# Outputs and forget gathers moved into attention's middle, the prefix scan cut into pieces, and the first RWKV loads issued during the last attention pair

## Chip, core and metric

The kernel runs on one core of one Trainium2 chip. The metric is the device time of one execution in microseconds (us); the time of a version is the median of its runs. Engines are named as in the profile: PE (matmul), PEld (its weight loads), DVE, ACT, POOL, SP (whose queue here only issues DMAs), and the core's 16 DMA engines.

## The reference

One step of a hybrid decoder layer with four mixers side by side. The prompt has 2048 tokens, the decode batch 8 sequences of 4 tokens with 8192 cached tokens each. What the change touches, cut to it:

```python
z = rmsnorm(x) @ w_in                       # 1024 -> all mixers' columns
logf = log_sigmoid(f_a + fox_bf)            # forget gate, 4 heads
# A, prompt: forgetting attention, query blocks of 128, causal
c = cumsum(logf)
p = softmax(q @ k.T * scale + c_q - c_k);  o_a = p @ v
# A, decode: the same over the paged cache
c = cumsum(concat(cache_logf[page_table], logf))     # 8192 + 4 per sequence and head
k_past, v_past = cache_k[page_table], cache_v[page_table]
# B, prompt: RWKV-7, a scan over 2048 tokens of a 64x64 state per head
# C pooling, D convolution
mixed = concat(o_a * silu(g_a), o_b * silu(g_b), o_c * ..., o_d * ...)
y = x + mixed @ w_out
# also returned: k, v, logf of the prompt and of the samples, shift rows, states
```

## The kernel before

Everything is float32. One program is written by hand for each engine; the order on an engine is the order of its code, and engines meet at semaphores that count up. SP and POOL issue DMAs in order: an instruction that waits holds back whatever is queued behind it. Most of SBUF is one tensor, cut into areas by offset, which the profile calls `big`; areas are used again by later stages, and that is what many of the waits are for. Other names there: `zst` (a staging area), `wbuf` (weights, later turned probabilities), `zT`, `rwS`, `rkv`, `ncD`, `mixT` (scratch in DRAM), `pidx`, `lidx` (indices of gathers).

The stages, in the time of the profiled execution:

- **0 to 855 us, projection.** PE computes z in slots (L766); the side branches (pooling, convolution, RWKV's preparation) run beside it on DVE, ACT and POOL.
- **855 to 1212 us, forgetting attention of the prompt.** 32 items j: 16 query blocks of 128 rows, for each block two pairs of heads. For item j PE does the scores (L905), in chunks of up to 512 keys; DVE adds the decays and takes the row maximum (`diagonal` L1795, `row_max` L1810 and L1816), negates it (`negate` L1830, which raises `s_max`); ACT takes the exponential with the row sum (`soft`, L1336); DVE makes a diagonal matrix of 1/sum (`scale_rows` L1834, L1836); PE turns the probabilities with it (L918, raises `p_tr`), ACT copies them out of PSUM (`turned`, L1448), PE multiplies them with the values (L929), and DVE multiplies the result by the gate (`finish` L1844, raises `o_read`, which therefore counts finished items). In each round of its loop DVE prepares item j+1 and finishes item j-1.
- **1212 to 1244 us, hand-over.** DVE does the prefix sum of the decode's forget gates (L1865), SP fetches key pages and the first RWKV pairs.
- **1244 to 1600 us, RWKV** in 8 pairs of 128-token chunks (PE L959), with 32 decode key steps between its products: `key_step(k)` multiplies 16 key pages with the decode queries `qbd`. SP's `key_pages(k)` (L525) issues the 16 pages of a step, 128 KB each, into a ring of three; `pair_load(n)` (L533, L534) loads pair n.
- **1600 to 2039 us**, decode state, softmax and values of decode attention (64 gathers of cache values by POOL, L727, four of which are issued at the end of the RWKV stage), output projection (L1267).

Around the start of attention. SP waits for the last projection slot, loads the gate of attention (`gate_a`, L499, 128 x 2080, twice), then the decays of keys from 512 on (`ck_rest`, L500), and then sends outputs: kT, v_prompt, v_sample, logf twice, shiftE (L502 to L510). POOL's 64 gathers of the cached forget gates (L727, `gather` of `lf_in`) wait for the value rows' projection and for `nc_kept`. They are indirect DMAs, each of a column of 128 numbers of 128 values. ACT copies the sample part of the gate into `gate_s` before item 0.

Around its end. SP waits for `o_read` 32 before it loads the page order (`pids`, L513), stores attention's output (`mixT`, L515), issues `key_pages(0)` and `key_pages(1)`, then two pair loads, then `key_pages(2)`. PE waits for `o_read` 32 before the first product of RWKV. DVE does four scans of 128 x 2048, waits for the stores of `mixT`, and builds three triangular masks from POOL's memsets, the zero state and `qbd`.

Of the kernel before, what the change touches and what calls it, by code (L numbers as in the profile page):

```python
# [7 lines left out]
ALU = mybir.AluOpType  # L8
# [3 lines left out]
P = 128  # L12
# [37 lines left out]
CH = 64  # L50
# [35 lines left out]
def build(nc, I, O):  # L86
    ctx = ExitStack()
    with ctx:
# [88 lines left out]
        EPS, IDENT, ONES, COUNTS, PADS, ONES_A, RMASKS = 4, 6, 11, 12, 16, 17, 25  # L177
# [67 lines left out]
        rows_ = [[area(6144 + h * SEQ, SEQ) for h in range(2)], [zst[:, h, 0:SEQ] for h in range(2)]]  # L245
# [14 lines left out]
        ck_rest = area(0, 4, SEQ - 512)  # L260
# [78 lines left out]
        mfull = area(HT + 8194, 2, P)  # L339
        mask = area(15168, 2, CH)  # L340
        mask_m = area(15296, CH)
        mrow = area(HT + 8450, P)
        id64 = area(HT + 12932, 64)
# [12 lines left out]
        id64_ready = sem("id64_ready")  # L356
# [28 lines left out]
        qbd = area(14656, 2, DEC_BATCH * 32)  # L385
# [67 lines left out]
        def _(sp):  # L453
# [28 lines left out]
            sp.dma_start(dmask, I['diag_mask']).then_inc(rows_in, 16)  # L482
            sp.dma_start(bf_b, I['fox_bf'].to_broadcast([P, 4])).then_inc(rows_in, 16)
# [43 lines left out]
            for k in range(2):  # L527
                key_pages(k)
            sp.wait_ge(mixa_stored, 32)

# [84 lines left out]
        def _(pool):  # L615
# [96 lines left out]
            for n, val in ((0, 1.0), (1, -1.0)):  # L712
                g.memset(mfull[:, n, :], val).then_inc(made, 1)
            g.memset(mrow[:, :], -1.0).then_inc(made, 1)
# [1513 lines left out]
```

## Time and profile before

| | us |
|---|---|
| median of 3 runs | 2035.19 |
| lowest, highest | 2031.91, 2035.75 |
| the profiled execution | 2041.06 |
| its span in the trace | 2039.3 |
| PE busy in it | 1801.3 (88%) |
| DVE, ACT, POOL busy | 818.4, 478.2, 173.4 |

The profile is of one execution, 5.9 us above the median. Its page gives the busy time by engine, the chain of work that ended last, and groups of instructions; the trace behind it gives stretches (tables with, each engine, busy us and count, then PE's granted clock as a share of full speed, the DMA engines' mean busy share, GB/s), and timelines, in which a bracket at a row's end tells how long the engine was idle before it and what ended that.

### The profile page before, as it was taken

How to read it: one execution, taken by the hardware profiler on the slowest of the kernel's cores; microseconds unless marked ns; L12 is line 12 of the kernel's file. 1: busy time of each engine (PE TensorE's matmuls, PEld its weight loads, DVE VectorE, ACT ScalarE, POOL GpSimd, SP SyncE). 2: the span in 40 equal slices, each digit the busy share in tenths (PEclk: the TensorE clock that was granted, in tenths of full speed). 3: DMA queues.
4: the chain of work that ended last, by engine and by line, in shares of the span. 5: the costliest groups of instructions: out<-in, count | busy, mean ns of one | idle time of the engine just before them, and what ended most of it. 6: DMA issues, size and time to landing. Idle time of an engine off the chain costs nothing.

```text
span 2039.3 us, 34632 instructions
## 1 busy us (share of the span) xinstructions
PE 1801.3 (88%) x14642; PEld 1097.0 (54%) x14642; DVE 818.4 (40%) x1661; ACT 478.2 (23%) x855; POOL 173.4 (9%) x228
## 2 busy tenths in 40 slices
PE   6999999999999999716999975878878776999997
PEld 3555555555545558404777764667766433444442
DVE  4350899531224510114554444444434684111111
ACT  4211100010553231203555541112111213100000
POOL 1000000110000000370000000000000001111120
PEclk9999999999999999957999997989989788999999
DMA  5232221655231550360000018677767607788872
GB/s 216 94 103 87 84 82 63 182 166 144 81 118 73 206 204 21 114 195 7 1 1 1 1 67 239 202 217 214 216 212 223 266 11 286 241 280 284 290 280 81
DMA packets 148692, 298.45 MB, mean 146 GB/s; under 512 B 23109, under 2 KB 119029, under 8 KB 129910
## 3 DMA queue, kind: packets, MB, share of 16 engines
q1 hardware_dynamic: 126026, 152.49, 23.6%
q0 software_dynamic: 18240, 115.82, 16.6%
q10 hardware_dynamic: 4272, 27.93, 3.3%
q8 instruction: 116, 1.90, 0.4%
q14 instruction: 38, 0.31, 0.0%
HBM read 234.50 MB, written 63.92 MB: 146 GB/s over the span
## 4 chain that ended last, share of the span: by engine, by line
PE 60%; SPq 15%; DVE 14%; issue 6%; ACT 2%; DMA 2%; another core or an unknown queue 2%; ACTq 0%; DVEq 0%
PE psum L766 24%; SPq L525 12%; PE psum L1267 12%; DVE big L1657 7%; PE psum L918 6%; PE psum L959 4%; PE psum L929 3%; PE psum L851 3%; PE psum L905 3%; SPq L521 2%; PE psum L798 1%; PE psum L1252 1%; DVE big L2039 1%; ACT big L1336 1%
## 5 line engine op out<-in xcount | busy, mean ns | idle before, releaser
L766 PE MATMUL psum<-big,wbuf 128*128 128x416 f32 x1920 | 675.1, 513 | 3.4 <-DVE big L1587 3.4
L766 PEld LDWEIGHTS psum<-big,wbuf 128*128 128x128 f32 x1920 | 365.2, 190 | 309.8 <-issue 307.8
L959 PE MATMUL psum<-big 64*64 64x64 f32 (+2 forms) x6496 | 270.0, 283 | 80.1 <-DMA big<-in_k_pages 32.2
L959 PEld LDWEIGHTS psum<-big 64*64 64x64 f32 (+1 forms) x6496 | 192.6, 134 | 169.0 <-issue 98.3
L1305 ACT ACTIVATE zst<-psum 128x416 f32<-128x416 f32 x125 | 64.0, 516 | 541.0 <-PE psum L766 535.8
L1267 PE MATMUL psum<-big 128*128 128x512 f32 (+1 forms) x408 | 180.9, 593 | 0.0
L1657 DVE SCALAR_TENSOR_TENSOR big<-big,pars 128x2048 f32<-128x2048 f32 x120 | 148.2, 1298 | 1.1
L727 POOL DMA_INDIRECT big<-in_cache_v,pidx x64 | 62.5, 976 | 1011.2 <-PE psum L959 1005.0
L929 PE MATMUL psum<-wbuf,big 128*64 128x128 f32 x544 | 77.2, 282 | 63.4 <-issue 35.0
L1267 PEld LDWEIGHTS psum<-big 128*128 128x128 f32 (+1 forms) x408 | 76.0, 186 | 100.8 <-issue 100.8
L2126 DVE TENSOR_TENSOR zst<-zst,psum 128x1024 f32<-128x1024 f32 (+1 forms) x17 | 20.7, 1220 | 224.1 <-PE psum L1267 224.1
L929 PEld LDWEIGHTS psum<-wbuf,big 128*64 128x64 f32 x544 | 57.9, 138 | 89.7 <-issue 52.6
L1565 ACT ACTIVATE big<-zst 128x1024 f32<-128x1024 f32 (+1 forms) x17 | 18.0, 1057 | 299.3 <-DVE zst L2126 299.3
L1267 PE MATMUL psum<-wbuf,big 128*128 128x512 f32 (+1 forms) x136 | 70.5, 643 | 16.7 <-DVE big L2101 15.5
L1448 ACT COPY wbuf<-psum 128x512 f32<-128x512 f32 (+3 forms) x80 | 41.4, 518 | 161.5 <-PE psum L918 108.1
L918 PE MATMUL psum<-big 128*128 128x128 f32 x544 | 72.3, 285 | 6.4 <-DVE big L1836 4.8
L929 PE MATMUL psum<-big 128*64 128x128 f32 x544 | 77.2, 282 | 0.0
L918 PE MATMUL psum<-big,zst 128*128 128x128 f32 x544 | 72.8, 286 | 3.9 <-DVE big L1836 3.4
L905 PE MATMUL psum<-big 64*128 64x512 f32 (+3 forms) x320 | 73.3, 569 | 0.6 <-ACT zst L1305 0.6
L918 PEld LDWEIGHTS psum<-big 128*128 128x128 f32 x544 | 64.8, 193 | 15.8 <-issue 6.6
L918 PEld LDWEIGHTS psum<-big,zst 128*128 128x128 f32 x544 | 65.2, 194 | 13.4 <-issue 5.9
L727 POOL DMA_INDIRECT big<-in_logf_rows,lidx x64 | 60.5, 945 | 126.4 <-DMA ncD<-big 107.2
(247 smaller groups left out, 1821.5 us busy)
## 6 DMA issues: line engine op xcount, KB each, us to landing
big<-in_k_pages SPq DMA_DIRECT2D x352, 128.0 KB, 2.3
zT<-zst ACTq DMA_DIRECT2D x25, 1040.0 KB, 6.5
zst<-in_k_pages SPq DMA_DIRECT2D x160, 128.0 KB, 2.4
wbuf<-in_w_slots SPq DMA_DIRECT2D x24, 512.0 KB, 4.5
big<-zT POOLq DMA_DIRECT2D x11, 1024.0 KB, 5.5
big<-zT SPq DMA_DIRECT2D x8, 1040.0 KB, 9.6
rwS<-big POOLq DMA_DIRECT2D x8, 1024.0 KB, 4.2
big<-rwS SPq DMA_DIRECT2D x8, 1024.0 KB, 5.7
```

The lines of the kernel that those rows point to most:

```text
L525: sp.dma_start(k_ring[k % NRING][:, n % DEC_BATCH, n // DEC_BATCH, :, :], I['k_pages'][bass.ds(page, 1)].rearrange("o p r c -> (o p) r c") ...
L727: g.indirect_dma_start(out=dst, out_offset=None, in_=cache, in_offset=bass.IndirectOffsetOnAxis(ap=idx, axis=0)).then_inc(s, 16)
L766: last = nc.tensor.matmul(psum[:, m % CHUNKS, 0:CW], w[:, k, :], hT[:, k, c * CW:(c + 1) * CW], start=(k == 0), stop=(k == KT - 1))
L851: last = nc.tensor.matmul(psum[0:r, 5 + n % 3, 0:VF], hT[:, k, n * P:n * P + r], wvf[:, k, :], start=(k == 0), stop=(k == KT - 1))
L905: last = nc.tensor.matmul(psum[:, 2 * (b % 2) + h, 0:w], kq[hs, 1, pr, i * P:(i + 1) * P], kq[hs, 0, pr, c * 512:c * 512 + w], start=True, ...
L918: last = nc.tensor.matmul(psum[:, 4 + h, k * P:(k + 1) * P], rows_[j % 2][h][:, x:x + P], diag[:, j % 2, h, :], start=True, stop=True)
L929: last = nc.tensor.matmul(psum[h * 64:h * 64 + 64, 6 + j % 2, 0:P], vtok[:, k, (2 * pr + h) * 64:(2 * pr + h + 1) * 64], probsT[h][:, k * ...
L959: return nc.tensor.matmul(out, l, r, start=start, stop=stop, skip_group_check=True)
L1267: last = nc.tensor.matmul(psum[0:n, 2 * u + o, :], l, wo[e][:, o * 512:(o + 1) * 512], start=(k == 0), stop=(k == 7))
L1305: nc.scalar.activation(zst[:, u, c * CW:(c + 1) * CW], psum[:, m % CHUNKS, 0:CW], f, scale=0.125 if n in (QA, QA + 1) else 1.0).then_inc(z ...
L1448: nc.scalar.copy(probsT[h][:, c * 512:c * 512 + width(j, c)], psum[:, 4 + h, 0:width(j, c)]).then_inc(pT_ready, 1)
L1657: last = v.scalar_tensor_tensor(out, in_, w, out, ALU.mult, ALU.add)
```

## The change

1. **Gate and decays (SP, ACT, DVE).** The load of `gate_a` is cut: columns 0 to 511 first, then `ck_rest`, then the rest, counted with `ck_rest` (48 instead of 16). ACT's copy of `gate_s` moves from before item 0 to item 8.
2. **Outputs (SP).** kT, v_prompt, v_sample, both logf and shiftE wait for `o_read` 12.
3. **Forget gathers (POOL).** All 64 wait for `o_read` 8.
4. **Prefix scan (DVE).** Eight scans of 1024 instead of four of 2048, one at the end of each round j = 20 to 27 of attention's loop, in place of the four after it.
5. **Hand-over (SP).** The page order and `key_pages(0)` come once all row maxima are there (`s_max` 32), `pair_load(0)` once all of item 30 is turned, `key_pages(1)` once all of item 31 is, then `o_read` 32, `pair_load(1)`, the stores of `mixT`, a copy of a mask, `key_pages(2)`. ACT and DVE no longer wait for the stores of `mixT` at RWKV's start (DVE does before it first writes `o_rw`), and PE waits for `o_read` 32 before `key_step(0)` and no longer before the first grams.
6. **Masks (SP, POOL, DVE).** RWKV's masks come by one DMA as an input, `rw_masks`; POOL's memsets and selects and DVE's three additions go. The zero state and `qbd` are made in the last round of DVE's loop, ahead of the two last `finish`. Some areas move to make room.

The order on SP, around the start of attention; before:

```order
L499 DMA big<-zT 128x2080 x2
L500 DMA big<-ncD 128x4x1536
L502 DMA out_kT<-zT 32x8320 x2
L504 DMA out_v_prompt<-big 128x16x256
L505 DMA out_v_sample<-big 32x256
L507 DMA out_logf_prompt<-big 128x16x4
```

and after:

```order
L499 DMA big<-zT 128x512 x2
L500 DMA big<-ncD 128x4x1536
L502 DMA big<-zT 128x1568 x2
L505 DMA out_kT<-zT 32x8320 x2
L507 DMA out_v_prompt<-big 128x16x256
L508 DMA out_v_sample<-big 32x256
```

The outputs keep their order behind `ck_rest`; the order does not show that a wait for 12 finished items now stands ahead of them.

The order on SP at the hand-over; before, from the second pair of loads on to the first row of `key_pages(2)` (32 key pages stand above these rows):

```order
L533 DMA big<-rwS 128x8x256
L534 DMA big<-rkv 128x2x256
L533 DMA big<-rwS 128x8x256
L534 DMA big<-rkv 128x2x256
L521 TENSOR_LOAD big
```

and after, from `pair_load(1)`:

```order
L530 DMA big<-rwS 128x8x256
L531 DMA big<-rkv 128x2x256
L541 DMA mixT<-big 128x2048 x2
L542 DMA big<-in_rw_masks 128x64
L522 TENSOR_LOAD big
```

`pair_load(0)` now stands between the pages of `key_pages(0)` and of `key_pages(1)`, and the stores of `mixT` have moved from ahead of all pages to behind `pair_load(1)`.

The order on DVE at the end of attention; before:

```order
L1834 RECIPROCAL linv<-lsum 128x2
L1836 TENSOR_SCALAR big<-ident,linv 128x128 x2
L1844 TENSOR_TENSOR big<-psum,big 128x128 x2
L1862 MEMSET big 128x1
L1865 SCALAR_TENSOR_TENSOR big<-big 128x2048 x4
L1870 MEMSET big 128x128
```

and one of the eight places after (round 20, where the scan's area is also set up):

```order
L1831 TENSOR_SCALAR big<-ident,linv 128x128 x2
L1844 MEMSET big 128x1
L1846 SCALAR_TENSOR_TENSOR big<-big 128x1024
L1790 TENSOR_TENSOR big<-big 128x256
L1805 ISA big<-psum,big 128x512
```

The scan stands between the diagonal matrices of an item and the first row maxima of the next.

The diff, cut:

```diff
@@ SP, start of attention
             for t in range(2):
                 sp.wait_ge(z_stored[1 - t], 16 * (11 + t))
-                sp.dma_start(gate_a[:, t, :], zT[GA + t]).then_inc(ga_in, 16)
+                sp.dma_start(gate_a[:, t, 0:512], zT[GA + t][:, 0:512]).then_inc(ga_in, 16)
             sp.dma_start(ck_rest, ...).then_inc(ck_in[1], 16)
+            for t in range(2):
+                sp.dma_start(gate_a[:, t, 512:], zT[GA + t][:, 512:]).then_inc(ck_in[1], 16)
+            sp.wait_ge(o_read, 12)
             for t in range(2):
                 sp.dma_start(O['kT'][t], zT[KA + t]).then_inc(st_stored, 16)
...
@@ SP, hand-over
-            sp.wait_ge(o_read, len(ITEMS))
             sp.wait_ge(st_stored, 16 * 7)
+            sp.wait_ge(s_max, len(ITEMS))
             sp.dma_start(pids[:, :], ...).then_inc(pids_in, 16)
-            for t in range(2):
-                sp.dma_start(mixT[MIX_A + t][:, 0:SEQ], gate_a[:, t, 0:SEQ]).then_inc(mixa_stored, 16)
             sp.wait_ge(pids_in, 16)
...
-            for k in range(2):
-                key_pages(k)
-            sp.wait_ge(mixa_stored, 32)
-            for n in range(2):
-                pair_load(n)
+            key_pages(0)
+            sp.wait_ge(p_tr, 2 * first_block[len(ITEMS) - 1])
+            pair_load(0)
+            sp.wait_ge(p_tr, 2 * first_block[len(ITEMS)])
+            key_pages(1)
+            sp.wait_ge(o_read, len(ITEMS))
+            pair_load(1)
+            for t in range(2):
+                sp.dma_start(mixT[MIX_A + t][:, 0:SEQ], gate_a[:, t, 0:SEQ]).then_inc(mixa_stored, 16)
+            sp.dma_start(id64_s, I['rw_masks'][:, 3 * CH:4 * CH]).then_inc(s_in, 16)
             key_pages(2)
+            sp.wait_ge(mixa_stored, 32)
@@ POOL
             pool.wait_ge(nc_kept, 16)
+            pool.wait_ge(o_read, 8)
             pool.wait_ge(f_copied, 2)
@@ PE
-            pe.wait_ge(o_read, len(ITEMS))
...
             def key_step(k):
                 if k == 0:
                     pe.wait_ge(qbd_ready, 1)
+                    pe.wait_ge(o_read, len(ITEMS))
@@ ACT
-            act.wait_ge(ga_in, 32)
-            a_(gate_s[:, :, :], gate_a[:, :, SEQ:T_ALL], ACT.Copy, gates)
             for j in range(len(ITEMS)):
+                if j == 8:
+                    act.wait_ge(ck_in[1], 48)
+                    a_(gate_s[:, :, :], gate_a[:, :, SEQ:T_ALL], ACT.Copy, gates)
...
-            act.wait_ge(mixa_stored, 32)
             rwkv_pair(0, 0, True)
@@ DVE
+            def forget_sums(n):
+                if n == 0:
+                    dve.wait_ge(lf_in, 16 * N_PAGES)
+                    ch.link(v.memset(scores_[:, 0:1], 0.0))
+                x = 1 + n * 1024
+                ch.link(v.tensor_tensor_scan(scores_[:, x:x + 1024], ones_a[:, 0:1].to_broadcast([P, 1024]), scores_[:, x:x + 1024],
+                                             0.0 if n == 0 else scores_[:, x - 1:x], ALU.mult, ALU.add))
...
                     negate(j + 1)
                     scale_rows(j + 1)
+                    if 20 <= j < 28:
+                        forget_sums(j - 20)
                 else:
+                    v.memset(state[:, 0, :], 0.0).then_inc(state_zero, 1)
+                    decode_queries()
                     finish(j - 1)
             finish(len(ITEMS) - 1)
-            dve.wait_ge(lf_in, 16 * N_PAGES)
-            ch.mark(v.memset(scores_[:, 0:1], 0.0))
-            for n in range(4):
-                x = 1 + n * 2048
-                ch.link(v.tensor_tensor_scan(scores_[:, x:x + 2048], ...))
-            dve.wait_ge(mixa_stored, 32)
-            dve.wait_ge(made, RMASKS)
...
```

## Rows read from the trace of the kernel before

**Rows 1.** Page, the chain that ended last, by engine.

```profile
PE 60%; SPq 15%; DVE 14%; issue 6%; ACT 2%; DMA 2%; another core or an unknown queue 2%; ACTq 0%; DVEq 0%
```

**Rows 2.** Stretches: PE, PEld, DVE, ACT, POOL busy (count), clock, DMA share, GB/s.

```profile
842.00:848.00 6.00, 6.00 (x18) 3.25 (x18) 0.00 (x0) 0.52 (x1) 4.40 (x5) 1.00 0.72 136
...
880.00:890.00 10.00, 0.00 (x0) 0.00 (x0) 0.68 (x4) 0.00 (x0) 7.56 (x9) 0.50 1.13 281
910.00:922.00 12.00, 0.00 (x0) 0.00 (x0) 0.73 (x6) 0.00 (x0) 9.26 (x10) 0.50 0.16 55
932.00:942.00 10.00, 8.86 (x56) 5.92 (x56) 5.55 (x32) 5.38 (x17) 0.00 (x0) 0.69 0.00 1
```

**Rows 3.** Timeline of PE, items 2 and 3 of attention.

```profile
898.78 0.47 PE L929 MATMUL psum<-wbuf,big 128*64 128x128 f32 x1 [27.17 <-issue]
...
932.50 0.47 PE L929 MATMUL psum<-wbuf,big 128*64 128x128 f32 x1 [28.36 <-ACT big L1448]
```

**Rows 4.** Timeline of POOL, first and last of the 64 forget gathers.

```profile
842.38 1.03 POOL L727 DMA_INDIRECT big<-in_logf_rows,lidx  x1 [107.19 <-DMA ncD<-big]
...
921.15 0.94 POOL L727 DMA_INDIRECT big<-in_logf_rows,lidx  x1 [0.30 <-issue]
```

**Rows 5.** Timeline of SP's queue, start and end of the burst.

```profile
853.90 0.82 SPq L499 DMA_DIRECT2D big<-zT  x2
...
887.85 0.50 SPq L510 DMA_DIRECT2D out_shiftE<-zT  x1
```

**Rows 6.** Timeline of DVE, the same place of two RWKV pairs.

```profile
1544.83 0.42 DVE L1934 TENSOR_TENSOR big<-big,psum 128x256 f32<-128x256 f32 x1 [0.61 <-PE psum L959]
...
1548.04 0.42 DVE L1941 TENSOR_TENSOR big<-big,psum 128x256 f32<-128x256 f32 x1 [1.85 <-PE psum L959]
...
1587.00 0.42 DVE L1934 TENSOR_TENSOR big<-big,psum 128x256 f32<-128x256 f32 x1 [0.47 <-PE psum L959]
...
1593.39 0.42 DVE L1941 TENSOR_TENSOR big<-big,psum 128x256 f32<-128x256 f32 x1 [3.63 <-PE psum L959]
```

**Rows 7.** Timeline of POOL, first of four value gathers there.

```profile
1586.33 0.94 POOL L727 DMA_INDIRECT big<-in_cache_v,pidx  x1 [664.24 <-PE psum L959]
```

**Rows 8.** Timeline of DVE: diagonals of items 2, 4, 5, finish of items 7 and 11.

```profile
869.10 0.41 DVE L1795 TENSOR_TENSOR big<-big 128x256 f32<-128x256 f32 x1
...
934.07 0.42 DVE L1795 TENSOR_TENSOR big<-big 128x256 f32<-128x256 f32 x1
...
938.52 0.42 DVE L1795 TENSOR_TENSOR big<-big 128x256 f32<-128x256 f32 x1
...
959.79 0.29 DVE L1844 TENSOR_TENSOR big<-psum,big 128x128 f32<-128x128 f32 x1
...
986.01 0.29 DVE L1844 TENSOR_TENSOR big<-psum,big 128x128 f32<-128x128 f32 x1
```

**Rows 9.** Timeline of DVE, last negated maximum (item 31) and last finish.

```profile
1192.20 0.17 DVE L1830 TENSOR_SCALAR nb<-big 128x2 f32<-128x2 f32 x1
...
1211.55 0.29 DVE L1844 TENSOR_TENSOR big<-psum,big 128x128 f32<-128x128 f32 x1 [11.49 <-PE psum L929]
```

**Rows 10.** Timeline of SP's queue at the hand-over.

```profile
1216.95 17.84 SPq L525 DMA_DIRECT2D big<-in_k_pages  x32
...
1242.05 9.67 SPq L525 DMA_DIRECT2D zst<-in_k_pages  x16
...
1254.03 6.30 SPq L525 DMA_DIRECT2D big<-in_k_pages  x11
```

**Rows 11.** Timeline of PE, first product of RWKV.

```profile
1243.67 6.68 PE L959 MATMUL psum<-big 64*64 64x64 f32 x128 [32.17 <-DMA big<-rkv]
```

**Rows 12.** PE's waits from 1240 to 1600 us: total, times, longest.

```profile
PE psum L959 <- DMA big<-in_k_pages: 32.2, 12, 4.8
```

**Rows 13.** Scans after attention, by line; DVE's idle time at one item.

```profile
L1865 DVE TENSOR_TENSOR_SCAN big<-big 128x2048 f32<-128x2048 f32 x4 | 17.9, 4469 | 0.1
...
1063.33 0.17 DVE L1834 RECIPROCAL linv<-lsum 128x2 f32<-128x2 f32 x1 [4.64 <-ACT zst L1336]
```

More of the change, by code:

```diff
@@ L176, in build @@
         made = sem("made")
-        EPS, IDENT, ONES, COUNTS, PADS, ONES_A, RMASKS = 4, 6, 11, 12, 16, 17, 25
+        EPS, IDENT, ONES, COUNTS, PADS, ONES_A = 4, 6, 11, 12, 16, 17
         rows_in = sem("rows_in")
@@ L244, in build @@
         gate_a = area(12480, 2, T_ALL)
-        rows_ = [[area(6144 + h * SEQ, SEQ) for h in range(2)], [zst[:, h, 0:SEQ] for h in range(2)]]
+        rows_ = [[area(h * SEQ, SEQ) for h in range(2)], [zst[:, h, 0:SEQ] for h in range(2)]]
         probsT = (wbuf[:, :, :, :].rearrange("p a b c -> p (a b c)"), area(10240, SEQ))
@@ L259, in build @@
         ck_first = area(HT + 21330, 4, 512)
-        ck_rest = area(0, 4, SEQ - 512)
+        ck_rest = area(4096, 4, SEQ - 512)
         diag = area(HT + 23378, 2, 2, P)
@@ L338, in build @@
         o_rw = area(10496, 2, T_ALL)
[L339 to L343, printed above, removed]
+        mask = area(HT + 8194, 2, CH)
+        mask_m = area(HT + 8322, CH)
+        id64 = area(HT + 8386, CH)
+        rw_masks = area(HT + 8194, 4 * CH)
+        id64_s = area(HT + 12932, CH)
         wkv_o = area(7200, 256)[0:CH]
@@ L354, in build @@
         gate_b = area(HT + 13000, 2, T_ALL)
-        id64_ready = sem("id64_ready")
         r_in = [sem("r_in0"), sem("r_in1")]
@@ L384, in build @@
         v_slot = area(HT + 17448, NSLOT, KV_ROW)
-        qbd = area(14656, 2, DEC_BATCH * 32)
+        qbd = area(HT + 13010, 2, DEC_BATCH * 32)
         aux = area(HT + 25640, P)
@@ L482, in _ @@
             sp.dma_start(dmask, I['diag_mask']).then_inc(rows_in, 16)
+            sp.dma_start(rw_masks, I['rw_masks']).then_inc(rows_in, 16)
             sp.dma_start(bf_b, I['fox_bf'].to_broadcast([P, 4])).then_inc(rows_in, 16)
@@ L711, in _ @@
             pool.wait_ge(rw_stored, 128)
-            for n, val in ((0, 1.0), (1, -1.0)):
-                g.memset(mfull[:, n, :], val).then_inc(made, 1)
-            g.memset(mrow[:, :], -1.0).then_inc(made, 1)
-            pool.wait_ge(made, ONES_A + 3)
-            for n in range(2):
-                g.affine_select(out=mfull[:, n, :], in_=mfull[:, n, :], compare_op=ALU.is_ge, fill=0.0, base=-n,
-                                pattern=[[1, P]], channel_multiplier=-1).then_inc(made, 1)
-            g.affine_select(out=mrow[:, :], in_=mrow[:, :], compare_op=ALU.is_ge, fill=0.0, base=-1,
-                            pattern=[[-1, P]], channel_multiplier=1).then_inc(made, 1)
-            pool.wait_ge(made, ONES_A + 6)
-            g.memset(mfull[0:64, :, 64:P], 0.0).then_inc(made, 1)
-            g.memset(mrow[64:P, 0:64], 0.0).then_inc(made, 1)
             pool.wait_ge(idx_ready, 1)
@@ L1844, in finish, with decode_queries @@
                 v.tensor_tensor(gate, psum[:, 6 + j % 2, 0:P], gate, ALU.mult).then_inc(o_read, 1)
+            def forget_sums(n):
[5 more added lines that the diff above has]
+                                             0.0 if n == 0 else scores_[:, x - 1:x], ALU.mult, ALU.add))
+            def decode_queries():
+                ch.link(v.memset(qbd[:, :, :], 0.0))
+                for h in range(4):
+                    pr, hs = h // 2, slice((h % 2) * CH, (h % 2) * CH + CH)
+                    to = qbd[hs, pr, :].rearrange("p (c e x) -> p c e x", c=4, e=2)
+                    of = qT_s[hs, pr, :].rearrange("p (c e q) -> p c e q", c=4, e=2)
+                    for e in range(2):
+                        x = e * 16 + h * 4
+                        ch.mark(v.tensor_copy(to[:, :, e, x:x + 4], of[:, :, e, :]))
+                ch.join()
+                dve.sem_inc(qbd_ready, 1)
             dve.wait_ge(ck_in[0], 16)
@@ L1997, in carry @@
                 at('o1', 2)
+                if isinstance(i, int) and i == 0 and before == 0:
+                    dve.wait_ge(mixa_stored, 32)
                 for s in range(2):
@@ L2016, in _ @@
             v.tensor_scalar(neg_m[:, :], m1[:, :], -1.0, None, ALU.mult).then_inc(D['neg'], 1)
-            dve.wait_ge(s_in, 32)
+            dve.wait_ge(s_in, 48)
             dve.wait_ge(s_dec, 1)
@@ L2205 @@
     given['aux'] = aux
+    c, q = p[:, None] % CH, np.arange(CH)[None, :]
+    given['rw_masks'] = np.concatenate([q >= c, -1.0 * (q > c), -1.0 * (q < c), q == c], axis=1).astype(np.float32)
     given['diag_mask'] = np.where(p[None, :] <= p[:, None], 0.0, -1e30).astype(np.float32)
```

24 lines of the change are left out of this document (3 added, 21 removed).

## The prediction

> **What bounds the kernel now.** I read the chain of waits first: PE carries 60% of it, SP's queue 15%, DVE 14% [rows 1]. So a microsecond counts where PE stands still, and in two places where SP's issuing sets the pace. Then I took the table of stretches around the two ends of attention, which the change touches, and looked for stretches with PE near zero.
>
> The first is at attention's start. From 842 to 848 us PE works 6.00 of 6.00 us at clock 1.00 though POOL already issues gathers; from 880 to 890 and from 910 to 922 it has no matmul at all, at 0.50, and from 932 it is back at 8.86 of 10 [rows 2]. PE's timeline shows two gaps, 27.17 and 28.36 us, ended by "issue" or by ACT [rows 3], and nobody there is truly busy: DVE has 0.7 us of work and ACT none [rows 2]. The reader should see what runs meanwhile. The 64 forget gathers go out from 842.38 to 921.15, 1.25 us apart [rows 4]; SP's burst of gate, decays and outputs is issued from 853.90 to 887.85 [rows 5]. In 910 to 922 the burst is over, the DMA engines are at 0.16, and only gathers remain, yet PE still does nothing [rows 2]; it recovers some 9 us after the last gather's issue. I read this as PE's products being late while gathers run. It is an inference: no row names the mechanism.
>
> In DVE's timeline the diagonals of items 2 and 4 start at 869.10 and 934.07, those of 4 and 5 at 934.07 and 938.52 [rows 8]: items 2 and 3 took 65 us where two items of 4.45 us take 9. **So the stall costs 56 us** (52 to 60, as one counts the items before and their natural pace).
>
> The second place is the hand-over. PE's first product of RWKV comes at 1243.67, 32.17 us after its last of attention [rows 11], when the pair loads land that SP queued behind 32 key pages of 17.84 us [rows 10]. Behind that, the RWKV stage waits for key pages, 32.2 us in 12 waits [rows 12]: the stage is bound by SP's stream of pages, so what counts is when that stream starts, not when PE does.
>
> **Part 1, attention's start.** Outputs and gathers leave it. What is left in the queues is the gate's first quarter, the decays and the rest of the gate, and no gathers. ACT no longer waits for the gate before item 0. Items 2 and 3 then run at the pace of their neighbours: **-56 us**. Finish of item 7 (o_read 8) moves from 959.79 to 904, and of item 11 from 986.01 to 930 [rows 8].
>
> **Part 2, the gathers again.** They now run from 904, 64 at 1.25 us, 80 us, to 984; nothing in the change makes them fewer or cheaper. What hid their first part before goes too: up to 853.9, about ten of them ran beside the last projection products, which lost nothing [rows 2, 4]. The outputs join at 930. The trace has two prices. (a) Items 2 and 3: 56 us were lost while the 54 gathers from 855 on were issued, 1.04 us each; 64 of them give 66 us. (b) Near the end of the RWKV stage, POOL issues four gathers of cache values, the first at 1586.33 [rows 7], and no output burst is there. Between the same two DVE instructions lie 3.21 us one pair earlier (1544.83 to 1548.04) and 6.39 us here (1587.00 to 1593.39) [rows 6]: 3.2 us for four, 0.8 each; 64 give 51 us. (c) If the stall begins only with the output burst, as the first one did about 4 us after the burst's start, it lasts from 934 to 993 (984 and the 9 us seen before), 59 us, less some 3 us of progress inside it: 56. Upper bound of the plain form: PE stands from the first gather to 9 us after the last, 89 us less 3. I take **+56 us**, which lies between (a) and (b) and is what (c) gives; own bounds 51 to 77.
>
> What the delayed work is needed for: the scans want all gathers at round 20, which comes at about 1063 [rows 13], less 56 and plus 56, well behind 993, and the pages' wait for the stored outputs is 200 us behind them. No new wait is late there. SP's wait for o_read 12 has only the outputs and the hand-over behind it; POOL's wait has the value gathers of 1586 behind it.
>
> **Part 3, the scan.** Before, four scans of 4.47 us, 17.9 in all [rows 13], lay after attention, beside SP's 32 pages, off the path. Now eight pieces of 2.24 us lie inside rounds 20 to 27. DVE is idle 4.64 us in such a round waiting for ACT's row sums [rows 13], more than a piece; but the piece comes just ahead of the next item's row maxima, which PE's later scores wait for, so up to some 0.6 us of it can come through where an item has four chunks of keys. Likeliest 0.25 us a piece, **+2 us**; 0 if all is hidden, 5 if each loses 0.6, 18 if all were on the path, which the idle time speaks against.
>
> **Part 4, the hand-over.** The page order is loaded once the last maximum is negated, at 1192.20 and not after the last finish at 1211.55 [rows 9]. From that point to the first page it takes some 5.4 us (last finish at 1211.55, first page at 1216.95 [rows 9, 10]). So, in the old clock: pages 0 from 1197.6, 16 times 0.56 us [rows 10], to 1206.5; pair 0 to 1207.5; the wait for item 31's turns to about 1209; pages 1 to 1218; pair 1 and the stores to 1223 (an estimate: five DMAs at 0.5 to 1 us each, and what a full queue adds); pages 2, with their register load, to 1234; pages 3 at about 1236, against 1254.03 [rows 10]. **-18 to -20 us; I take -20.** It cannot be more than 32 (the whole gap [rows 11]), and the late SP queue could leave 12. DVE's masks and PE's wait for o_read 32 cost nothing on the path: the additions and memsets are a few tenths of a us each. qbd now comes ahead of two finishes, some 2 us of DVE, inside an idle time of 11.49 us [rows 9]. Loading pages during the last item could slow its products; the last stall of this kind came with gathers, and these are ordinary loads, such as ran beside the projection at a DMA share of 0.72 and PE at 6.00 of 6.00 [rows 2]; I take 0.
>
> **Sum.** -56 + 56 + 2 - 20 = -18 against the profiled execution's 2041.06, so 2023; its span is 2039.3, and it lies 5.9 us above the median of the runs. Taken from the median: 2035.2 - 18 = **2017**. Own range of this case: -56 + 51 + 0 - 28 = -33 at best; with the upper ends, -56 + 77 + 5 - 20 = +6, so 2002 to 2041.
>
> **Rivals.**
>
> A, *no stall in the middle.* The stall of before belongs to the meeting of gathers with the burst at the very start of attention, where DMA work was at 1.01 to 1.13 of what the engines take, or to small items; in the middle PE's items are longer and the gathers pass unseen, as those of 842 to 848 did [rows 2]. Then -56 + 0 + 2 - 20 = -74: **1961** (1949 to 1973). Against it: the 12 us with DMA at 0.16 and PE at zero [rows 2], and the four gathers at 1586 [rows 6, 7].
>
> The Trainium skill, "SBUF — State Buffer", section "Who interferes with whom", says that PE and ACT never wait on anyone for SBUF and that a DMA never contends with a compute engine. By that rule the gathers could not slow the products in the middle of attention, and the time would be rival A's. This case's trace speaks against it as far as it goes: no matmul in 880 to 890 and 910 to 922 [rows 2] with DVE and ACT nearly idle.
>
> B, *slower than before: a full stop over all 64 gathers.* Before, ten gathers were hidden under projection work, and then two small items were all that waited. If PE stops for the whole 904 to 993, the middle costs 89 - 3 = 86, and with the queue late at the hand-over (12): -56 + 86 + 2 - 12 = +20, **2055**. It decides where PE loses more than about 74 us between 904 and 993 with the hand-over at its likeliest, or 66 with 12. For it: in 910 to 922 the gathers alone gave a full stop. Against it: the price of 0.8 at the four value gathers.
>
> C, *the hand-over gives nothing, the rest as forecast.* RWKV's pace is set by the pages, but if a page's landing, not its issue, is what counts, or the pages of the last item only shorten a wait that comes back at the ring's third slot, -18 becomes +2: 2037. It is the upper end of the forecast's own range with a small chance.
>
> **Chances.** Forecast, stall of 51 to 77 us in the middle with a hand-over gain: 0.60. A: 0.27. B: 0.09. C: 0.04. Within the forecast's own case, about 0.12 of all lies within 0.2% (4 us, about what a measurement of this kernel can tell from no change) or just above, together with C. This gives faster 0.73 (A's 0.27 and 0.46 of the forecast's), same 0.12, slower 0.15 (B's 0.09 and the forecast's upper end, 0.06). The range takes in A down to 1952 and the upper ends of the forecast and C, up to 2046; B and the tail of A stay out.
>
> **What the profile of the changed kernel would show.** Part 1: diagonals of items 2 to 5 some 4.4 us apart, no gap of over 10 us on PE before 900. Part 2: gathers from about 904 to 984, and between 930 and 993 gaps of tens of us on PE at clock 0.50; right if the eight or so items there cost 50 to 77 us more than before. If PE's work there is unbroken, A holds; if it is broken from 904 on, B. Part 3: scan pieces of about 2.24 us, DVE's idle time at the reciprocals shrunk by them, the item pace within 0.6 us of before. Part 4: first page issued about 5 us after the last negated maximum, PE's gap at the hand-over down from 32 us to under 8, `key_pages(3)` about 24 us after the last finish, against 42 before. The forecast would be wrong above all if the stall is not tied to gathers, or if it costs PE by the gather and not by time.

## The result, and the profile after

The changed kernel takes **2042.75 us** (median of 5 runs, 2041.08 to 2045.36), the kernel before beside it 2031.91 (2030.6 to 2035.75, 5 runs): ratio 1.0049, 95% interval 1.0034 to 1.0064. It is slower by 11 us where 18 us of gain were forecast. The two profiled executions differ by less, 2041.39 against 2041.06; the one of before lies 9 us above the median it has here, so the traces show well where time goes and comes from, and the sum of the terms less well.

Attention's start is free now, and its middle is not. Stretches of the changed kernel, columns as in [rows 2]:

```profile
855.00:900.00 45.00, 32.95 (x244) 23.09 (x242) 25.63 (x142) 22.03 (x61) 1.30 (x2) 0.85 0.36 141
900.00:930.00 30.00, 10.62 (x76) 6.98 (x72) 6.03 (x28) 3.75 (x10) 22.89 (x24) 0.75 0.16 53
930.00:960.00 30.00, 0.00 (x0) 0.00 (x0) 1.82 (x12) 0.00 (x0) 22.70 (x24) 0.50 0.16 52
960.00:990.00 30.00, 5.73 (x28) 4.28 (x30) 0.00 (x0) 2.81 (x7) 14.19 (x15) 0.50 0.11 35
```

From 930 to 960 PE has no matmul, the DMA share is 0.16, and beside POOL only DVE has 1.82 us of work: the picture of [rows 2], 910 to 922, and this time without any output burst before it. PE's gaps there, and POOL's first and last forget gather (timelines):

```profile
963.85 1.22 PE L913 MATMUL psum<-big 128*128 128x128 f32 x4 [47.05 <-issue]
985.49 1.23 PE L913 MATMUL psum<-big 128*128 128x128 f32 x4 [20.42 <-ACT big L1443]
```

```profile
898.40 1.03 POOL L721 DMA_INDIRECT big<-in_logf_rows,lidx  x1 [165.00 <-DVE big L1839]
...
977.74 0.95 POOL L721 DMA_INDIRECT big<-in_logf_rows,lidx  x1 [0.30 <-issue]
```

What PE's rows leave out shows in the rows of those who wait for it. The score products of item 11, and the row maximum on DVE that reads them (timelines):

```profile
907.66 1.56 PE L900 MATMUL psum<-big 64*128 64x512 f32 x8
...
923.39 0.69 DVE L1805 CUSTOM_DVE_ANT_0 zst<-psum,big 128x512 f32<-128x512 f32 x1 [13.06 <-remote]
```

DVE starts on the first head 15.7 us after the products' row begins, and on the second at 930.96; in a trace without the stall (e8, below) it starts the same step 2.3 us after that row. The turned probabilities recorded from 910.05 on are copied by ACT (L1443) only at 963.21, and PE's next row follows that copy. So a row of PE is not yet a result: in this stall the last products before the gap are recorded in time and their results come late, and PE then waits for engines that wait for it. Whether PE works late or only reports late, no row tells. "PE stops" below is meant in this sense.

DVE's diagonals give the pace, as in [rows 8]. Those of items 9 and 12:

```profile
895.02 0.42 DVE L1790 TENSOR_TENSOR big<-big 128x256 f32<-128x256 f32 x1
...
991.48 0.42 DVE L1790 TENSOR_TENSOR big<-big 128x256 f32<-128x256 f32 x1
```

Before, the diagonal of item 9 came at 957.69 and that of item 12 at 976.31. So the start gave 62.7 us, and items 9 to 11 took 96.5 us instead of 18.6: **77.9 us lost, not 56**. From the diagonal of item 20 to that of 31 the changed kernel takes 147.6 us, before 140.5: **7.1 us** for the eight scan pieces, not 2.

SP's queue at the hand-over (timeline), beside [rows 10]; the last finish is now at 1233.60:

```profile
1217.17 8.65 SPq L526 DMA_DIRECT2D big<-in_k_pages  x16
...
1232.86 9.12 SPq L526 DMA_DIRECT2D big<-in_k_pages  x16
...
1250.41 10.30 SPq L526 DMA_DIRECT2D zst<-in_k_pages  x16
...
1263.02 19.43 SPq L526 DMA_DIRECT2D big<-in_k_pages  x32
```

`key_pages(3)` (last row) is issued 29.4 us after the last finish, before 42.5. PE's first product of RWKV (L953, at 1234.19) comes 0.63 us after its last of attention, where it came 32.17 us after it [rows 11]. From the last finish to the end of the span it is 806.0 us, before 827.8: about 22 us gained. The ledger of the two traces: -62.7 + 77.9 + 7.1 - 22 = +0.3, which is what their spans differ by.

### The profile page after: what moved, and what is told of

Same layout as the page of the kernel before. It is cut to its first block, busy times and chain, and to the rows that moved or that the text cites. A ratio compares the mean times of both kernels' runs of the same rounds, so it can differ in the third digit from the quotient of the medians.

```text
span 2039.6 us, 34625 instructions
## 1 busy us (share of the span) xinstructions
PE 1810.0 (89%) x14642; PEld 1097.8 (54%) x14642; DVE 818.2 (40%) x1662; ACT 478.9 (23%) x855; POOL 172.6 (8%) x220
## 4 chain that ended last, share of the span: by engine, by line
PE 58%; DVE 15%; SPq 14%; issue 4%; another core or an unknown queue 4%; ACT 3%; DMA 1%; ACTq 0%; DVEq 0%
PE psum L761 25%; PE psum L1262 12%; SPq L526 12%; DVE big L1652 7%; PE psum L913 6%; PE psum L953 4%; PE psum L846 3%; PE psum L924 2%; PE psum L900 2%; SPq L522 2%; ACT big L1331 1%; PE psum L793 1%; PE psum L1247 1%; DVE big L2033 1%
## 5 line engine op out<-in xcount | busy, mean ns | idle before, releaser
L953 PE MATMUL psum<-big 64*64 64x64 f32 (+2 forms) x6496 | 271.5, 283 | 50.4 <-DMA big<-in_k_pages 32.0
L953 PEld LDWEIGHTS psum<-big 64*64 64x64 f32 (+1 forms) x6496 | 191.4, 134 | 142.3 <-issue 72.9
L1443 ACT COPY wbuf<-psum 128x512 f32<-128x512 f32 (+3 forms) x80 | 41.5, 519 | 175.6 <-PE psum L913 118.7
```

Source lines behind the costliest of these rows:

```text
L953: return nc.tensor.matmul(out, l, r, start=start, stop=stop, skip_group_check=True)
L1443: nc.scalar.copy(probsT[h][:, c * 512:c * 512 + width(j, c)], psum[:, 4 + h, 0:width(j, c)]).then_inc(pT_ready, 1)
```

## The experiments

The kernels of a group ran on the same chip, beside the kernel before. The kernel before turned out to need very different times on different chips, so each group is named by its chip. Each chip was used for one group only: what is called a difference of chips here could also be a passing state of the chip. The chip of the result above is not on record.

| chip | before there | kernels |
|---|---|---|
| A | 2038.2 | e1 to e4 |
| B | 1977.6 | e5 to e8 |
| C | 2042.4 | r1, e9, r2, r3 |
| D | 2040.3 | x1 to x4 |
| E | 1975.2 | y1, y2 |

**e1_gathers_early: are the outputs needed for the stall?**

```diff
             pool.wait_ge(nc_kept, 16)
-            pool.wait_ge(o_read, 8)
```

> The changed kernel with POOL's wait for eight finished items taken out, so that the 64 forget gathers run from about 842 to 922 as before, while the outputs stay late. If the gathers alone halt PE whenever attention runs beside them (theory G), PE stops from about 858 to 930 as before, and the middle runs free: the middle's 78 us go, the start's 60 come back, so about 18 to 22 us less than the changed kernel, 2020 to 2025 us. If the output burst was needed for the stall at the start (theory B), the start stays free too: about 60 to 75 us less, 1965 to 1980 us.

2028.77 us (2025.16 to 2032.0), ratio to before 0.9953 (0.9932 to 0.9974). From the diagonal of item 1 to that of item 4 it takes 76.4 us (858.4 to 934.8), exactly as before (857.67 to 934.07), though no output is sent until item 12. The output burst had no part in the stall. Beside the gathers there are still SP's loads of gate and decays here, and in the changed kernel's middle not even those. The time is 4 us above the 2020 to 2025 expected of this case.

**e2_plain: is it the DMA traffic, or the gathers' kind?**

```diff
-                gather(scores_[:, x:x + PAGE], cf, lidx[:, t:t + 1], lf_in)
+                g.dma_start(scores_[:, x:x + PAGE], cf[t * 32:t * 32 + P]).then_inc(lf_in, 16)
```

> The changed kernel with each of the 64 indirect gathers replaced by a plain DMA of the same shape and destination from POOL's queue, 128 rows of 512 B (the forget gates read are then the wrong pages). If it is the indirect gathers that halt PE (G), the middle loses nothing: 70 to 78 us less than the changed kernel, about 1968. If it is the DMA writes of 64 KB into SBUF themselves, whoever issues them, PE loses the same and the time stays within 10 us of 2043.

1968.52 us (1962.91 to 1970.91), ratio 0.9645 (0.9625 to 0.9666). This kernel fetches the wrong pages' forget gates; everything else is as in the changed kernel. 64 transfers of the same 64 KB, from the same queue at the same place, 0.53 us apart and not 1.25, leave PE at work. The stretch while they run:

```profile
900.00:935.00 35.00, 34.09 (x298) 25.68 (x298) 20.06 (x102) 20.10 (x44) 33.90 (x64) 1.00 0.54 163
```

PE is busy 34.09 of 35 us at three times the data rate of the gathers. Items 9 to 11 take 18.6 us, to the tenth as before the change.

**e3_spread: four gathers after each item.**

```diff
-            pool.wait_ge(o_read, 8)
+                if t % 4 == 0:
+                    pool.wait_ge(o_read, 1 + t // 4)
```

> The changed kernel with the 64 gathers spread over items: four gathers after each of the first 16 finished items instead of all after the eighth. If PE loses a fixed time for each gather (0.8 to 1.2 us), the sum is the same 51 to 78 us and the time is 2015 to 2043. If the loss comes from gathers following one another at once (a backlog), four at a time cost little: 1970 to 2000.

1980.49 us (1974.7 to 1987.47), ratio 0.9725. From the diagonal of item 1 to that of item 20 it takes 134.9 us, e2_plain 122.2: 12.7 us for the 64 gathers, 0.2 each, where back to back they cost 1.2.

**e4_scan_after: the scan pieces behind the last finish.**

```diff
-                    if 20 <= j < 28:
-                        forget_sums(j - 20)
...
             finish(len(ITEMS) - 1)
+            for n in range(8):
+                forget_sums(n)
```

> The changed kernel with the eight scan pieces back behind the last finish. If the pieces inside rounds 20 to 27 cost the 7 us that the two traces differ by there, and 18 us of scans after attention are hidden beside the first RWKV work, the time is 7 us less, 2036. If the scans then delay the first RWKV products on DVE, which now start at once, up to 18 us come back: 2043 to 2054.

2038.8 us (2033.85 to 2041.79), ratio 1.0006, between the two times expected. Items 20 to 31 take 140.5 us again. The scans run for 19 us behind the last finish, and the part from there to the end is 2.8 us longer than in the changed kernel (808.8 against 806.0). The changed kernel did not run on this chip, so the net, about 4 us for the old place, rests on the two traces.

**e5, e6, e7: on chip B.** e5 adds 30 gathers back to back during the projection to e3_spread; e6 issues eight after every second item; e7 one at a time:

```diff
+            for t in range(30):
+                x = 6272 + t * PAGE if t < 15 else 2176 + (t - 15) * PAGE
+                gather(scores_[:, x:x + PAGE], cf, lidx[:, t:t + 1], xtra)
+            pool.wait_ge(xtra, 480)
...
-                if t % 4 == 0:
+                if t % 8 == 0:
...
-                if t % 4 == 0:
-                    pool.wait_ge(o_read, 1 + t // 4)
+                pool.wait_ge(p_tr, 1 + t * 58 // 64)
```

> The kernel with four gathers after each of 16 items (e3_spread), plus 30 more gathers of the same kind issued back to back while PE does projection or value rows, before attention (their data is overwritten by the real gathers). If a run of back-to-back gathers stops PE wherever it works once some ten are queued (a backlog, theory Q), PE loses 20 to 30 us there and the time is 2000 to 2010. If PE is only stopped in attention (theory A, something in attention's own code), the time stays at 1980, within 5 us.

> As e3_spread, but eight gathers after every second item instead of four after each. Theory Q with its threshold near ten (the stop set in 10 to 13 gathers after the first, in both traces): still mostly free, 1980 to 1990. If the cost grows with the length of a group from the start, about 0.6 us each: 2000 to 2010.

> As e3_spread, but one gather at a time, each waiting for one more chunk of turned probabilities (from item 1 on, done by item 19). If each gather costs PE about 0.2 us whatever its neighbours (12.6 us for 64 in e3_spread), the time stays at 1978 to 1984. If what was left in e3_spread came from the groups, it falls by up to 12, to 1968.

1962.89, 1966.32 and 1964.67 us, before 1977.59 there. None of the expectations could be tried: on this chip the gathers do not stop PE. Items 1 to 20 take 122.9, 122.1 and 122.7 us, as in e2_plain, however the gathers are grouped.

**e8_old_handover: the changed kernel with SP's old order, on chip B.**

```diff
-            sp.wait_ge(s_max, len(ITEMS))
+            sp.wait_ge(o_read, len(ITEMS))
             sp.dma_start(pids[:, :], ...)
+            for t in range(2):
+                sp.dma_start(mixT[MIX_A + t][:, 0:SEQ], gate_a[:, t, 0:SEQ]).then_inc(mixa_stored, 16)
             sp.wait_ge(pids_in, 16)
...
             key_pages(0)
-            sp.wait_ge(p_tr, 2 * first_block[len(ITEMS) - 1])
+            key_pages(1)
+            sp.wait_ge(mixa_stored, 32)
             pair_load(0)
-            sp.wait_ge(p_tr, 2 * first_block[len(ITEMS)])
-            key_pages(1)
-            sp.wait_ge(o_read, len(ITEMS))
             pair_load(1)
-            for t in range(2):
-                sp.dma_start(mixT[MIX_A + t][:, 0:SEQ], gate_a[:, t, 0:SEQ]).then_inc(mixa_stored, 16)
             sp.dma_start(id64_s, I['rw_masks'][:, 3 * CH:4 * CH]).then_inc(s_in, 16)
             key_pages(2)
```

> The changed kernel with SP's order at the hand-over put back: page order, stores of the output, key pages 0 and 1, both pair loads and key pages 2 all behind the last finish. If the new hand-over is worth what the two traces show from the last finish on (the span differs by +0.3 where the last finish is 22 us later), the time is 20 to 24 us longer than the changed kernel, about 2064. If the stage recovers by itself (the ring of pages catches up), under 10 us.

1978.67 us (1975.48 to 1981.06), ratio 0.9999, 12 to 16 us above its three neighbours, which have the new hand-over. The expected 20 to 24 us over the changed kernel can't be read here, as that one did not run on this chip. It also has all 64 gathers back to back in attention's middle, as the changed kernel, and here is what they do on this chip:

```profile
900.00:930.00 30.00, 29.01 (x247) 21.11 (x248) 16.52 (x85) 17.68 (x39) 22.27 (x23) 1.00 0.25 81
930.00:960.00 30.00, 29.98 (x279) 23.74 (x276) 17.29 (x78) 16.91 (x29) 22.82 (x24) 1.00 0.68 170
960.00:990.00 30.00, 30.00 (x266) 22.47 (x265) 15.69 (x72) 16.50 (x31) 16.37 (x18) 1.00 0.13 40
```

POOL's share is the same 22.8 of 30 us, and PE works without a break at clock 1.00. Diagonals of items 9 and 12: 897.5 and 916.1, 18.6 us apart. The four value gathers near the end of the RWKV stage show the same. Between the two DVE instructions of [rows 6] there lie here (timeline)

```profile
1531.26 0.42 DVE L1924 TENSOR_TENSOR big<-big,psum 128x256 f32<-128x256 f32 x1 [0.43 <-PE psum L951]
...
1534.24 0.42 DVE L1931 TENSOR_TENSOR big<-big,psum 128x256 f32<-128x256 f32 x1 [2.02 <-PE psum L951]
```

2.98 us and not 6.39, with the gathers issued at 1530.63 to 1534.37.

**r1_after: the changed kernel, unchanged, on chip C.**

> The changed kernel once more, since the kernel before takes about 2035 us on one chip and 1978 us on another. Theory C (the stall is a property of some chips): on a chip where before takes about 1978, attention's middle runs free and the change is worth its hand-over less its scan pieces, 12 to 16 us, so 1962 to 1966; on a chip where before takes about 2035, the middle stalls again and the time is 2038 to 2045. Rival: the changed kernel is slower on every chip, then 1985 to 1990 on the first kind.

2046.57 us (2041.59 to 2050.57), ratio 1.0025 (1.0012 to 1.0038): a chip with the stall, and slower there again, by 4 us (2038 to 2045 was expected).

**e9_scan_in_idle: e7_singles with the scan piece ahead of `scale_rows`.**

```diff
-                    scale_rows(j + 1)
                     if 20 <= j < 28:
                         forget_sums(j - 20)
+                    scale_rows(j + 1)
```

> The changed kernel with single gathers (e7_singles) and each scan piece placed ahead of an item's diagonal matrices and not behind them, where DVE waits 4.4 to 4.6 us for ACT's row sums. If the 7 us that the pieces cost come from delaying the next item's row maxima, rounds 21 to 29 run as before the change and the time is 7 us below e7_singles on a chip without the stall, 1956 to 1959; on a chip with the stall 1960 to 1975. If the pieces cost by contention and not by place, nothing changes.

1966.31 us (1961.77 to 1968.48), ratio **0.963** (0.9608 to 0.9651). Items 20 to 31 take 140.5 us: the pieces cost nothing. DVE's timeline shows why; first the changed kernel, then e9, one round each:

```profile
1078.27 0.17 DVE L1829 RECIPROCAL linv<-lsum 128x2 f32<-128x2 f32 x1 [4.64 <-ACT zst L1331]
...
1079.01 2.29 DVE L1846 TENSOR_TENSOR_SCAN big<-big 128x1024 f32<-128x1024 f32 x1
1081.34 0.43 DVE L1790 TENSOR_TENSOR big<-big 128x256 f32<-128x256 f32 x1
```

```profile
1050.39 2.35 DVE L1846 TENSOR_TENSOR_SCAN big<-big 128x1024 f32<-128x1024 f32 x1
1055.64 0.17 DVE L1829 RECIPROCAL linv<-lsum 128x2 f32<-128x2 f32 x1 [2.91 <-ACT zst L1331]
1056.24 0.42 DVE L1790 TENSOR_TENSOR big<-big 128x256 f32<-128x256 f32 x1
```

The idle time lies ahead of the reciprocal. Behind it the piece pushes back the next diagonal and the row maxima; ahead of it it only shortens the wait from about 4.6 to 2.9 us.

**r2_z_extra and r3_groups8: e5 and e6 again, on chip C.**

> The kernel with four gathers after each item and 30 more gathers back to back during projection, for a chip with the stall: if back-to-back gathers stop PE everywhere there, the stretch 745 to 795 us grows by 20 to 30 us and the time is 2000 to 2010; if only attention is stopped, it stays at 1980. On a chip without the stall: 1963 again, and nothing is told.

> Eight gathers after every second item, for a chip with the stall: if the stop sets in only after some ten gathers, 1980 to 1990 us; if the cost grows with each gather that follows another at once, 2000 to 2010. On a chip without the stall: 1966 again.

2001.42 us (2000.19 to 2007.12) and 2021.61 (2013.11 to 2026.76). The 30 extra gathers run from 747.0 to 784, and PE in the value rows' products (L852) falls away after 15 to 20 of them. Stretches of r2_z_extra, and of e5_z_extra on chip B:

```profile
755.00:765.00 10.00, 10.00 (x30) 5.44 (x29) 0.00 (x0) 0.52 (x1) 7.56 (x9) 1.00 0.26 81
765.00:775.00 10.00, 7.38 (x33) 5.95 (x32) 0.00 (x0) 0.52 (x1) 7.56 (x9) 1.00 0.36 126
775.00:785.00 10.00, 2.74 (x5) 1.33 (x5) 0.00 (x0) 0.00 (x0) 7.16 (x8) 0.55 0.26 86
785.00:795.00 10.00, 8.10 (x22) 5.76 (x22) 0.00 (x0) 1.09 (x3) 0.00 (x0) 0.60 0.02 7
```

```profile
765.00:785.00 20.00, 20.00 (x93) 17.36 (x92) 0.00 (x0) 2.32 (x6) 13.21 (x14) 1.00 0.27 97
```

Attention then starts some 17 us later than its neighbours (first diagonal 868.1 against 850.7 to 851.7); on chip B the same 30 gathers delay nothing (848.8 in e5). The stop is not a thing of attention's code: it comes in the projection stage too, with a delay. In r3_groups8 items 1 to 20 take 175.6 us, 53.4 more than in e2_plain: 0.83 us for each gather in groups of eight. The expected threshold near ten is wrong; the cost grows with the length of a group. (Whether a group of eight is long enough by itself, or meets what the one before it left behind, these runs don't tell apart.)

| gathers issued | lost over e2_plain's pace | for each |
|---|---|---|
| one at a time (e9) | 6.1 us | 0.1 |
| groups of 4 (e3) | 12.7 | 0.2 |
| groups of 8 (r3) | 53.4 | 0.83 |
| 64 at once (changed kernel) | 77.6 | 1.2 |

The loss is counted over items 1 to 20. It is not a matter of the mean rate: r3's gathers are spread over 135 us, e3's over 106 and e9's over 113. The four come from different chips with the stall, so small differences between rows mean little.

**x1_quarter_rows: the instruction, or the rows it fetches?**

```diff
+                if t == 0:
+                    g.memset(scores_[:, :], 0.0).then_inc(xtra, 1)
+                    pool.wait_ge(xtra, 1)
-                gather(scores_[:, x:x + PAGE], cf, lidx[:, t:t + 1], lf_in)
+                gather(scores_[0:32, x:x + PAGE], cf, lidx[0:32, t:t + 1], lf_in)
```

> The changed kernel with each of the 64 gathers fetching 32 rows instead of 128, into an area that POOL first sets to zero (three quarters of the forget gates are left out). On a chip with the stall: if what halts PE is POOL's gather instruction, whose count and spacing stay, the middle still loses some 78 us, 2043; if it is the rows (packets) that the gathers put into the queue, a quarter of them costs a quarter or, below the threshold of a backlog, nothing: 1968 to 1990. On a chip without it: 1965 either way.

2055.94 us (2055.23 to 2057.11), ratio 1.0086 (1.0056 to 1.0115); x4_after beside it 2050.8. A quarter of the rows, and PE stands as before:

```profile
915.00:960.00 45.00, 4.92 (x16) 3.69 (x16) 0.65 (x3) 0.00 (x0) 33.42 (x39) 0.52 0.05 14
960.00:1000.00 40.00, 5.48 (x32) 4.12 (x32) 3.98 (x21) 3.66 (x8) 14.09 (x17) 0.52 0.02 7
```

The diagonals of items 10 and 12 are 93.2 us apart, 12.7 before. (Three quarters of the forget gates are left out.) At 14 GB/s and a DMA share of 0.05 it is not the traffic; what has stayed is the number and the spacing (1.17 us) of POOL's gather instructions. The 5 us over x4_after come with POOL's memset at the start: it runs from 896.97 for 6.93 us, and a DVE instruction that takes 0.17 us elsewhere (negated maximum, L1829) takes 6.90 beside it, from 897.03 on. The diagonals of items 9 and 10 are 12.0 us apart, in x4 5.9.

**x2_best, x3_best_old_handover, x4_after: on chip D.** x2 is e9 again, x3 is x2 with SP's order as in e8, x4 the changed kernel.

> The version with single gathers and scan pieces in DVE's idle time. On a chip without the stall 1956 to 1959, about 20 below the kernel before (7 from the scan's place, 14 from the hand-over); on one with it 1962 to 1970 as measured.

> x2_best with SP's order at the hand-over as before the change, everything behind the last finish. If the hand-over is worth on this chip too what it was worth on the chip of e8 (14 us against its neighbours there), 14 us more than x2_best. If it is worth the 22 us by which the two traces differ from the last finish on, 20 to 24 more.

> The changed kernel beside these. On a chip where the kernel before takes about 1978 (theory C): 1962 to 1966, faster than before; where it takes about 2035: 2040 to 2047. On no chip should both stall and no stall show.

1967.93 us (1966.46 to 1970.28; ratio 0.9658, 0.9628 to 0.9687), 1984.74 (1981.99 to 1988.03) and 2050.8 (2047.61 to 2053.57; ratio 1.0059, 1.0033 to 1.0084). **The hand-over is worth 16.8 us** by the medians, between the 14 and the 20 to 24 expected, and 19.5 us from the last finish on between the two traces; `key_pages(3)` is issued 27.9 us after the last finish in x2 and 44.3 in x3.

**y1_reversed and y2_best: on chip E.** y1 issues the gathers in reverse order of pages, so that the first scan pieces need half of them, over items 1 to 21; y2 is e9.

```diff
-                pool.wait_ge(p_tr, 1 + t * 58 // 64)
+                pool.wait_ge(p_tr, 1 + k * 80 // 64)
```

> x2_best with the gathers in reverse order of pages, so that the first scan pieces need only the first half of them, and spread over items 1 to 21 instead of 1 to 19 (one per 1.25 chunks of turned probabilities). If what is left of the gathers' cost (6 to 9 us over items 1 to 19, most of it in items 16 to 19, where the gathers come every 1.6 us) is the POOL instructions' closeness, 3 to 5 us less than y2_best on a chip with the stall; on one without it, nothing. If each gather costs the same wherever it is, no change on either.

> x2_best again beside y1_reversed: 1962 to 1970 us on a chip where the kernel before takes about 2035, 1956 to 1959 where it takes about 1978 (theory C, so far shown there only by kernels other than this).

1955.9 us (1951.85 to 1960.96) and 1954.45 (1954.14 to 1958.14), before 1975.21 there. Again a chip without the stall, so what the wider spread would save on the other kind stays open. y2_best is faster than the kernel before on this kind of chip too, by 21 us: 0.9902 (0.9883 to 0.992).

## Why the prediction was wrong

**The views and what bounds the kernel: right.** Both places where PE stood were found, and their cause, gathers and SP's stream of pages, is what the runs show.

**The sum.** By the terms of the two traces it is -62.7 + 77.9 + 7.1 - 22 = +0.3, where -56 + 56 + 2 - 20 = -18 was forecast: 18.3 us of the miss, of which the middle made 21.9 and the scan 5.1, less 6.7 and 2 that start and hand-over gave in excess. The other 10.5 us up to the measured +10.8 are in no term; 9.2 of them are the height of the traced execution of before above its median. That 2042.75 still lies below the forecast's outer end of 2046 is owed to the width taken for the upper ends and rival C, not to the mechanism.

**Part 1, the start: right, size 62.7 for 56.** It also took in what items 0 and 1 gained (diagonals 2 and 1 are 6.0 us apart, before 11.4).

**Part 2, the gathers in the middle: this is the step that failed.** It was taken at +56 and measured +77.9 in the trace (77.9 in r1 and 79.7 in x4). Three things in it were wrong. Price (c), the one chosen, lets the stall begin only with the output burst; e1 shows that the burst has no part, and the changed kernel's stall sets in at 905 to 916, long before any output. Price (b), 0.8 us from four gathers at the end of the RWKV stage, cannot be multiplied by 64: the price of a gather runs from 0.1 to 1.2 us with the number that follow one another. And the ten gathers beside the last projection products cost nothing because the stop sets in late, not because projection is immune; r2 shows projection stopped as well. Moved into the middle, all 64 in a row are one long group: the stop begins after 5 to 14 of them and ends 7 us after the last. The prediction had this as rival B, with 86 us of loss and a point of decision at about 74, and gave it 0.09; its time of 2055 was too high, since it took only 12 us for the hand-over. The row that should have ruled was the one it quoted itself: no matmul from 910 to 922 with gathers alone [rows 2]. A stretch in which one thing runs and PE does nothing prices that thing at its full time.

**Part 3, the scan: the mechanism right, the size not.** 7.1 us for 2; the upper end was set at 5. The idle 4.64 us of [rows 13] was counted as cover, but it lies ahead of the instruction where DVE waits for ACT, and the piece was put behind it. Idle time covers only what stands before the wait that ends it; e9 moved one line, and items 20 to 31 take the old 140.5 us again.

**Part 4, the hand-over: right.** 20 forecast, 16.8 measured on chip D, 22 between the traces. PE's gap fell from 32.17 to 0.63 us, under the 8 expected; `key_pages(3)` came 29.4 us after the last finish, not 24. The stage is bound by the stream of pages, and rival C, that nothing would come of it, is out.

**Rival A, no stall in the middle, is what two of the chips do.** The changed kernel itself was not run there; e5, e6 and e7, which differ from it in how the gathers are grouped (and e5 in its 30 more), take 1963 to 1966 where before takes 1978. Its 1961 comes near, though by luck: it counts a stall of 56 us at the start as saved. On those chips the kernel before is 61 to 67 us faster than on A, C and D. It was not traced there, so that it has no stall at its start is inferred from this time; the gain is then the hand-over less the scan pieces. The Trainium skill, "SBUF — State Buffer", section "Who interferes with whom", has PE and ACT never waiting on anyone. Chip B agrees (PE 29.98 of 30 us beside 24 gathers in e8); in the changed kernel, with 0.00 of 30, something does hold PE up beside gathers, and there the measurement decides. The page speaks of SBUF, and no run here shows that SBUF is what PE waits for.

**Open.** Why POOL's gather instruction halts PE on three of the five chips and not on the other two, and whether that is lasting there; what in the instruction does it; whether PE's work or only its report is late. Excluded are its bytes and rows (x1), the outputs (e1), plain DMAs from the same queue (e2) and attention's code (r2). That PE waits for its own instructions was not tested, and the traces speak against it: the next 16 KB packet of the DMA queue of kind `instruction` starts 4 us after the diagonal of item 12 both in the changed kernel (995.7), where PE has been back for 10 us, and in e8 (920.4). Nor do the terms explain the whole 11 us of this result: r1 and x4 gave 4 and 10 for the same change.

## What to carry to other kernels

A burst of indirect gathers is not background work: issue them singly, each behind a step of the compute it runs beside, and not in one run behind one wait. Here that, together with the rest of the change and the scan piece moved in front of the wait that idles its engine, makes 2042 into 1966 us on a chip with the stall and 1975 into 1954 on one without it (there the grouping itself makes no difference). Before moving a stall's suspected cause elsewhere, price it by the stretch in which it runs alone. And where a profile shows an engine idle, look at when those who wait for it see its results.

## What the runs showed of the hardware

- **The same kernel takes 1975 to 1978 us on two chips and 2032 to 2042 on the others.** What differs is whether PE goes on while POOL issues gathers: items 9 to 11 of attention take 18.6 us (e8) or 96.5 to 98.3 us (changed kernel, r1, x4) beside the same 64 gathers. (For the kernel before this is an inference, as its only trace is of the slower kind.)
- **While it is stopped, PE is not dead but very slow, and its results come late.** Score products recorded at 907.66 are read by DVE at 923.39, turned probabilities recorded from 910.05 on by ACT at 963.21 (changed kernel). The trace of x1 has 16 matmuls, 4.92 us of them, in the 45 us from 915 to 960, at a granted clock of 0.52; in the changed kernel PE is back 7 us after the last gather.
- **An indirect gather of 32 rows holds PE up as much as one of 128** (0.87 and 0.94 us of POOL each; 93.2 us for items 10 and 11 against 12.7), a plain DMA of the same shape not at all (e2, 34.09 of 35 us of PE).
